# The MLP's moving operands stored in interleaved runs of 128 columns

## What is computed

```python
h = h + concat([ret_out, mla_out]) @ w_o
m = rmsnorm(h, norm_mlp_g)
h = h + square(relu(m @ w_up)) @ w_down
return rmsnorm(h, final_norm_g)
```

## Time and profile before

| what | value |
|---|---|
| median of the runs | 1194.4 us |
| lowest, highest | 1194.34, 1195.76 us |
| span of the profiled execution | 1192.3 us |
| TensorE busy | 1152.4 us (97%), 6758 matmuls |
| VectorE busy | 736.5 us (62%) |
| ScalarE busy | 609.2 us (51%) |
| GpSimd busy | 154.3 us (13%) |
| DMA | 206.33 MB, mean 173 GB/s |
| mean granted TensorE clock | 0.986 |

### The profile page before, as it was taken

How to read it: one execution, slowest core, us unless ns; L and a number is a source line. 1 busy time by engine, 2 the same in 40 slices (tenths; PEclk the granted TensorE clock), 3 DMA queues, 4 the chain that set the end, 5 groups by cost and what they waited for, 6 DMA issues and landing times.

```text
span 1192.3 us, 18902 instructions
## 1 busy us (share of the span) xinstructions
PE 1152.4 (97%) x6758; PEld 1004.7 (84%) x6758; DVE 736.5 (62%) x962; ACT 609.2 (51%) x942; POOL 154.3 (13%) x167
## 2 busy tenths in 40 slices
PE   2999999999998999999999999999999999999995
PEld 2897898888887888888888888888888888888884
DVE  7786767677768667666665444445666665444443
ACT  4454565555556556555554444444555554444441
POOL 5011111111113331000000111111000000111111
PEclk7999999999999999999999999999999999999997
DMA  7443433333415554554555555455455445544531
GB/s 295 183 163 133 168 133 132 132 145 128 167 71 216 190 193 176 187 200 177 182 201 180 177 199 187 176 184 198 183 177 200 185 177 189 198 176 180 204 109 70
DMA packets 29260, 206.33 MB, mean 173 GB/s; under 512 B 3376, under 2 KB 3376, under 8 KB 5680
## 3 DMA queue, kind: packets, MB, share of 16 engines
q1 hardware_dynamic: 28080, 199.66, 46.4%
q10 hardware_dynamic: 1152, 6.29, 1.4%
HBM read 203.84 MB, written 2.10 MB: 173 GB/s over the span
## 4 chain that ended last, share of the span: by engine, by line
PE 95%; DVE 3%; ACT 1%; DMA 1%; issue 0%; DVEq 0%; SPq 0%; ACTq 0%
PE acc L289 86%; PE ps_qn L289 3%; PE ps_qr L289 2%; DVE xs L845 1%; PE ps_y L289 1%; PE ps_v L289 1%; PE ps_x L289 1%; PE ps_kn L289 1%; DMA x_in<-x_all 1%; DVE res L828 0%; DVE lo L828 0%; ACT xs L591 0%; DVE hid L1089 0%; DVE mla_o L828 0%; ACT hi L546 0%
## 5 line engine op out<-in xcount | busy, mean ns | idle before, releaser
L828 DVE TENSOR_TENSOR lo<-raw,hi 128x1024 fp32r<-128x1024 f32 x366 | 450.3, 1231 | 245.0 <-ACT hi L546 240.7
L289 PE MATMUL acc<-xs,hi 128*128 128x512 f32 (+1 forms) x1952 | 589.3, 365 | 0.0
L546 ACT ACTIVATE hi<-raw 128x1024 fp32r<-128x1024 f32 x366 | 386.6, 1057 | 234.5 <-PE acc L289 228.4
L289 PE MATMUL acc<-xs,lo 128*128 128x256 f32 (+1 forms) x1648 | 457.9, 286 | 22.2 <-DVE xs L845 22.2
L289 PE MATMUL acc<-hid,hi 128*128 128x512 f32 x1280 | 450.8, 400 | 3.2 <-DVE hid L1089 3.2
L289 PEld LDWEIGHTS acc<-xs,hi 128*128 128x128 f32 x1952 | 346.7, 190 | 51.6
L289 PE MATMUL acc<-hid,lo 128*128 128x256 f32 x1280 | 352.3, 281 | 0.0
L289 PEld LDWEIGHTS acc<-xs,lo 128*128 128x128 f32 x1648 | 312.3, 190 | 31.3 <-DVE lo L828 9.1
L289 PEld LDWEIGHTS acc<-hid,hi 128*128 128x128 f32 x1280 | 238.1, 189 | 59.5 <-DVE hid L1089 4.5
L289 PEld LDWEIGHTS acc<-hid,lo 128*128 128x128 f32 x1280 | 242.5, 189 | 4.7
L546 ACT ACTIVATE half_b<-acc 128x256 f32<-128x256 f32 x132 | 50.7, 384 | 216.7 <-PE acc L289 216.7
(11 more groups left out here) (175 smaller groups left out, 621.0 us busy)
## 6 DMA issues: line engine op xcount, KB each, us to landing
raw<-w_up SPq DMA_DIRECT2D x64, 1024.0 KB, 4.8
raw<-w_down SPq DMA_DIRECT2D x64, 1024.0 KB, 4.8
raw<-w_in SPq DMA_DIRECT2D x38, 1024.0 KB, 4.8
raw<-w_o SPq DMA_DIRECT2D x16, 1024.0 KB, 4.8
side<-w_side ACTq DMA_DIRECT2D x8, 768.0 KB, 5.8
x_in<-x_all SPq DMA_DIRECT2D x4, 544.0 KB, 7.7
res<-x_frames SPq DMA_DIRECT2D x1, 2048.0 KB, 7.6
out<-res SPq DMA_DIRECT2D x2, 640.0 KB, 3.0
```

Of the source, the lines that this page charges most:

```text
L289: return pe.matmul(o, l, m, start=start, stop=stop)
L546: return act.activation(o, i, ACT.Copy)
L828: return dve.tensor_tensor(o, a, b, op)
```

## The change

The MLP gets its own views of the same memory: `xm` over `xs`, `hidm` over `hid`. Both have the shape [pairs of rows, 4, 2, 128]. Row `k` of old is now row `k // 2` and place `k % 2` of the third axis; the second axis holds hi of frames 0 to 127, hi of frames 128 to 255, and the same for lo. So a row's four runs of 128 columns lie 256 columns apart, and the runs of its neighbour lie between them. The 512-column matmul of the MLP reads four runs of 128 in place of two of 256 (up) or one of 512 (down), the 256-column one reads two of 128 in place of one of 256. ScalarE and VectorE write each 128x256 result as two runs of 128. The output in PSUM covers the same addresses as before. The output projection and everything ahead of it read `xs` and `hid` as before. Number and order of the instructions, waits and DMAs are unchanged.

```diff
+        here[0] = xs_at
+        xm = place("xm", [KT // 2, 4, 2, P], F32R)
+        here[0] = hid_at
+        hidm = place("hidm", [HALF_F // 2, 4, 2, P], F32R)
...
+        def tokens(t):
+            return t.rearrange("p (s t) -> p s t", s=2)
+        def part_hi(t, row, j):
+            return t[:, row, 0:2, j, :]
+        def part_lo(t, row, j):
+            return t[:, row, 2:4, j, :]
...
-            def wide(c, b, wide_of, hi_of, more=0, bmore=0, first=True, last=True, order=None, ready=None):
+            def wide(c, b, wide_of, hi_of, more=0, bmore=0, first=True, last=True, order=None, ready=None, runs=2):
                 a = acc[b % 2]
+                both = a[:].rearrange("p (a t) -> p a t", a=runs)
+                second = a[:, FRAMES:] if runs == 2 else a[:, FRAMES:].rearrange("p (a t) -> p a t", a=runs // 2)
...
-                        mm(a[:, FRAMES:], wl, hi_of(k), False, False)
-                    m = mm(a[:].rearrange("p (a t) -> p a t", a=2), wh, wide_of(k), first and n == 0, end)
+                        mm(second, wl, hi_of(k), False, False)
+                    m = mm(both, wh, wide_of(k), first and n == 0, end)
...
-                    wide(c0 + j, b0 + j, x_wide, x_hi, more, more, ready=ready)
+                    wide(c0 + j, b0 + j, lambda k: xm[:, k // 2, :, k % 2, :], lambda k: part_hi(xm, k // 2, k % 2),
+                         more, more, ready=ready, runs=4)
...
-                        wide(cd + DOWN_PER_BLOCK * n + part, bd + n, lambda k: hid_wide(part * KT + k),
-                             lambda k: hid_hi(part * KT + k), more, bmore, first=part == 0,
-                             last=part == DOWN_PER_BLOCK - 1, ready=up_parts if guard else None)
+                        wide(cd + DOWN_PER_BLOCK * n + part, bd + n,
+                             lambda k: hidm[:, (part * KT + k) // 2, :, k % 2, :],
+                             lambda k: part_hi(hidm, (part * KT + k) // 2, k % 2), more, bmore, first=part == 0,
+                             last=part == DOWN_PER_BLOCK - 1, ready=up_parts if guard else None, runs=4)
...
-                act.activation(xs[:, j, META:TOK], res[:, j, :], ACT.Identity,
+                act.activation(part_hi(xm, row, j0 % 2), tokens(res[:, j, :]), ACT.Identity,
                                scale=gain(G_MLP + j)).then_inc(sem["m_hi"], 1)
...
-                    act.activation(hid[:, n, 0:FRAMES], r[:], ACT.Square).then_inc(sem["up_hi"], 1)
+                    act.activation(part_hi(hidm, row, j0 % 2), tokens(r[:]), ACT.Square).then_inc(sem["up_hi"], 1)
...
-                dve.scalar_tensor_tensor(out=xs[:, j, TOK + META:], in0=res[:, j, :], scalar=gain(G_MLP + j),
-                                         in1=xs[:, j, META:TOK].bitcast(F32), op0=ALU.mult,
+                dve.scalar_tensor_tensor(out=part_lo(xm, row, j0 % 2), in0=tokens(res[:, j, :]), scalar=gain(G_MLP + j),
+                                         in1=part_hi(xm, row, j0 % 2).bitcast(F32), op0=ALU.mult,
...
-                    tt(hid[:, n, FRAMES:], sq[:], hid[:, n, 0:FRAMES].bitcast(F32), ALU.subtract).then_inc(sem["up_lo"], 1)
+                    tt(part_lo(hidm, row, j0 % 2), tokens(sq[:]), part_hi(hidm, row, j0 % 2).bitcast(F32),
+                       ALU.subtract).then_inc(sem["up_lo"], 1)
```

More of the change, by code:

```diff
@@ L120, in hymba_block @@
         lo = [place(f"lo{i}", [W], F32R) for i in range(2)]
+        xs_at = here[0]
         xs = place("xs", [KT, 2 * TOK], F32R)
@@ L136, in hymba_block @@
         rest_at = here[0]
+        here[0] = xs_at
+        xm = place("xm", [KT // 2, 4, 2, P], F32R)
+        assert here[0] <= hid_at
+        here[0] = hid_at
+        hidm = place("hidm", [HALF_F // 2, 4, 2, P], F32R)
+        assert here[0] <= res_at
         here[0] = hid_at + 2 * KT * TOK * 4
@@ L305, in wide @@
                     if end:
-                        mm(a[:, FRAMES:], wl, hi_of(k), False, False)
-                    m = mm(a[:].rearrange("p (a t) -> p a t", a=2), wh, wide_of(k), first and n == 0, end)
+                        mm(second, wl, hi_of(k), False, False)
+                    m = mm(both, wh, wide_of(k), first and n == 0, end)
                     if not end:
-                        m = mm(a[:, FRAMES:], wl, hi_of(k), False, False)
+                        m = mm(second, wl, hi_of(k), False, False)
                     if n % 8 == 7:
@@ L765, in _, with wo_block @@
             ret_round(g)
-            def wo_block(j, j0, more=0):
+            def wo_block(j, row, j0, more=0):
                 wide_block(C_WO + j0, C_WO + j0, W_WO + j0, more)
@@ L776, in _, with up @@
                 for j in range(4):
-                    wo_block(4 * i + j, j, 4 * i)
+                    wo_block(4 * i + j, 2 * i + j // 2, j, 4 * i)
             for half in range(2):
                 c0, b0, w0 = C_MLP + half * C_HALF, C_MLP + half * B_HALF, W_MLP + half * B_HALF
-                def up(n, j0, more=0, root=False):
+                def up(n, row, j0, more=0, root=False):
                     wide_block(c0 + j0, b0 + j0, w0 + j0, more)
@@ L793, in _ @@
                 for j in range(4):
-                    up(j, j, root=half == 0 and j == 0)
+                    up(j, j // 2, j, root=half == 0 and j == 0)
                 with act.Fori(1, HALF_F // 4) as i:
                     for j in range(4):
-                        up(4 * i + j, j, 4 * i)
+                        up(4 * i + j, 2 * i + j // 2, j, 4 * i)
                 cd, bd, wd = c0 + HALF_F, b0 + HALF_F, w0 + HALF_F
@@ L1122, in residual, with wo_block @@
                 tt(res[:, n, :], acc[b % 2][:, 0:FRAMES], t2[:], ALU.add).then_inc(sem["acc_read"], 1)
-            def wo_block(j, j0, m=0):
+            def wo_block(j, row, j0, m=0):
                 split_lo(C_WO + j0 + 2, 0, m)
@@ L1134, in _, with up @@
                 for j in range(4):
-                    wo_block(4 * i + j, j, 4 * i)
+                    wo_block(4 * i + j, 2 * i + j // 2, j, 4 * i)
             for half in range(2):
                 c0, b0, w0 = C_MLP + half * C_HALF, C_MLP + half * B_HALF, W_MLP + half * B_HALF
-                def up(n, j0, m=0, root=False):
+                def up(n, row, j0, m=0, root=False):
                     split_lo(c0 + j0 + 2, 0, m)
```

## The result

The changed kernel takes 1198.59 us, the median of six runs (1197.71 to 1199.29), beside 1194.89 us before. The ratio is 1.0031, with a 95% interval from 1.0019 to 1.0042: it became 0.3% slower, where 1.7% faster was forecast, and lies just outside the forecast's range.

The account below looks back on a forecast made before the run. The MLP was taken to go at the pace of TensorE's matmul pairs. Savings of 8.6 us (up stage) and 11.5 us (down stage), 20.1 us in all, with writes and supply at nothing, gave 1174 us, range 1165 to 1198.

Parts of the forecast that it names:

- What bounds the kernel: MLP, 60% of the time: goes at the pace of TensorE's matmul pairs; 1 ns a pair is 2.05 us.
- the price of a break: MLP's moving operands: each further break saves 2.8 ns, three a pair in the up stage, four in the down stage.
- The forecast of 342 ns: Both MLP stages: a pair falls from 350.4 and 353.1 ns to about 342 ns, 20.1 us less in all.
- The fit: Narrow chunks against down-stage pairs: 1.4 ns a matmul and 0.456 ns a column, so the excess goes with unbroken runs' columns.
- The rival that came true: MLP: addresses, not the break, made the up stage faster; no change to +2.8 us, 1194 to 1197 us; chance 0.12.
- The writes: ScalarE's square and VectorE's subtraction in two runs: taken at nothing, at most 0.6 us more work, under wide cover.
- The isolated gap: Skill page's N / 2.4 + 2.5 ns a matmul, 325 ns a pair; alone it would make the time unchanged.

Follow-up runs that it names:

- the forms: Kernels with the computation left out, TensorE alone running 64 matmuls or pairs of each operand layout; flat form and four runs of 128 took 353.1 or 346.7 ns a pair.
- up_two_runs_apart: The changed kernel with the up stage's operand as two runs of 256, all hi rows and then all lo rows; 1197.6 us, ratio 1.0028 to before.

## Why the prediction was wrong

**What bounds the kernel** was right. The MLP goes at the pace of its pairs, 1 ns a pair is 2 us, no engine or DMA took part, and TensorE alone shows the same paces.

**The step that failed** is the price of a break: "Its nearest row is the difference between the stages, the same form with one break more: -2.7 ns". The 2.7 ns were real but belonged to the addresses: at the old row distance the up stage keeps 350.4 ns with four runs, and at distances of 256 columns it has 353.1 ns with its old two. The price of a break, which I had put at -2.8 ns, is nothing in three places where one run is measured against four with rows 512 apart: 706.32 us for both in the kernel, 353.1 ns and 346.7 ns in the forms. The forecast of 342 ns was seven breaks times a difference that had another cause.

**The fit** of 1.4 ns a matmul and 0.456 ns a column came from forms with different addresses, and so had no meaning; the text warned of that and used it all the same for "nearly all of the excess goes with the columns". Against it, matmuls of 256, 320, 384 and 512 columns, each kind alone with rows 512 apart, have the same excess, 13.3 ns (120.0, 146.7, 173.3 and 226.7 ns). Only 448 columns have 20.0, and with rows 544 apart 272 columns have 10.0. The last argument for the forecast, that an excess which grows with an unbroken run must shrink when the run is halved, falls with it.

**The rival that came true** is the first one, in size as well: up to the down stage's pace, 1024 x 2.7 = 2.8 us, 1197 us. I gave it 0.12. What I held against it, that the narrow chunks on the same rows have the down stage's excess, was no evidence, since their starts and their run of 272 give them other places relative to the tiles. It was also called "no change" with an upper end of 1197. The step was of that size, but the six executions stand 3.7 us above those before, not 2.8, and the 0.9 us outside the MLP, which *up_two_runs_apart* does not show, took the median to 1198.6 and out of the range.

**The writes** in two runs cost nothing, as predicted: the square into `hid` takes 401 ns and the subtraction 418 ns in the second up stage, beside 402 and 420. The isolated gap of 2.5 ns a matmul beyond its columns that the Trainium skill gives ("TensorE: Matmul & The Clock Gate", section "Back-to-back issue gap") was met by none of these `float32r` forms; the nearest is 10.0 ns, for 272 columns alone.

**What stays open.** That the excess comes of weight loads meeting the moving operand's reads in the memory fits all this (it depends on their relative place, on history, and not on the other engines) but is only argued: no run shows the collision itself, or why some distances are good, or what decides which pattern an execution falls into. The wide form of the old up stage, slower alone and faster in its pair, is not explained either.

## What to carry to other kernels

Where two stages with the same arithmetic differ by some ns a matmul, count every way in which their operands differ before giving the difference to one of them; here the shape was the visible one and the address the effective one. Forms run alone can tell them apart, if each is run more than once behind different forms: one form here gave 353.3 ns in one program and 346.7 in the next. When TensorE bounds a `float32r` kernel, try some shifts of 4 or 8 columns of the moving operands against each weight buffer before changing a layout: one gap of 32 bytes, with rows 512 apart in both stages, was worth 1.3% here. Look at the single times, too: a kernel whose executions fall into two groups may be one pattern away from a better time.

## What the runs showed of the hardware

- A pair of `float32r` matmuls (768 columns) took 353.3, 351.7, 350.0, 348.1, 346.7 or 344.6 ns at a granted clock of 1.00 throughout, by the relative place of operand and tiles and by what went before. With rows 512 apart, one run, two of 256 or four of 128 made no difference.
- At the lower clock level the excess was not there. In the timeline of the kernel before, three 272-column matmuls take 32.62 - 31.94 = 0.68 us, just 816 columns at 1.2 GHz, while the window shows a granted clock of 0.50; at 1.00 they take 34.05 - 33.67 = 0.38 us, where 816 columns at 2.4 GHz are 0.34 (the windows' columns are those of the windows above):

```profile
31.94 0.43 PE L289 MATMUL acc<-xs,lo 128*128 128x272 f32 x1
...
32.62 0.43 PE L289 MATMUL acc<-xs,lo 128*128 128x272 f32 x1
...
33.67 0.29 PE L289 MATMUL acc<-xs,lo 128*128 128x272 f32 x1
...
34.05 0.29 PE L289 MATMUL acc<-xs,lo 128*128 128x272 f32 x1
```

```profile
31.90:33.30 1.40, 1.40 (x9) 1.40 (x7) 1.40 (x2) 0.00 (x0) 0.00 (x0) 0.50 0.00 0
33.70:36.00 2.30, 2.30 (x21) 2.30 (x20) 2.30 (x3) 1.06 (x1) 0.00 (x0) 1.00 0.39 57
```

- One program, with the same data, ran at 346.7 ns a pair in one profiled execution and at 353.3 in another, over the output projection and the whole MLP. The granted clock was 1.00 in both. Of its 16 times 11 lie within 1182.1 to 1186.1 us and 5 within 1197.5 to 1198.8, 1.2% apart.
